# Weight tiles in three buffers instead of two, and the first output projection by halves of the sequence

## The reference, cut to what matters

```python
# block 1 (even): conformer convolution and a gated linear recurrence
z = h @ w_in;  va, vg, ga, xb, gb = split(z)
y_a = silu(layernorm(depthwise_conv31(va * sigmoid(vg)))) * silu(ga)
y_b = rglru(xb) * silu(gb)
x = x + gate * (concatenate([y_a, y_b]) @ w_out)       # w_out: 2048 x 1024
h = modulate(rmsnorm(x))
# block 2 (odd): multiscale pooling, grouped projection, output projection in two parts; rmsnorm
# block 3: gated linear attention, output projection, a gated projection of p ("ple")
# block 4 (fox): q, k, v, g = split(h @ w_in), 16 heads of 64;
logits = q.k / 8 + c[t] - c[s], causal;  o = softmax(logits) @ v, * silu(g), output projection, ple
```

## Time and profile before

| | |
|---|---|
| median of 3 runs | 3277.76 us (3275.65 to 3282.16) |
| the profiled execution | 3278.82 us, of which the profile's span is 3277.1 us |
| PE busy | 3028.1 us, 92% |
| DVE, ACT, POOL busy | 1759.4, 1061.4, 1216.6 us |
| granted TensorE clock | 0.965 of full speed |

### The profile page before, as it was taken

How to read it: one execution, slowest core, us unless ns; L and a number is a source line. 1 busy time by engine, 2 the same in 40 slices (tenths; PEclk the granted TensorE clock), 3 DMA queues, 4 the chain that set the end, 5 groups by cost and what they waited for, 6 DMA issues and landing times.

```text
span 3277.1 us, 39825 instructions
## 1 busy us (share of the span) xinstructions
PE 3028.1 (92%) x13850; PEld 2299.4 (70%) x13850; DVE 1759.4 (54%) x2248; ACT 1061.4 (32%) x1356; POOL 1216.6 (37%) x1466
## 2 busy tenths in 40 slices
PE   7999999979979999989889999998999999998997
PEld 1588777747868877767678877776666666665775
DVE  2499999984163415363632232445455555556353
ACT  3244334440021100000322232224455556655332
POOL 0244445414434433435423233675211212121575
PEclk9999999989989999989899999999999999998999
DMA  8212111243211131113211112333322122211323
GB/s 327 94 55 77 61 61 61 67 162 127 70 33 52 45 135 52 45 35 119 90 59 32 33 33 88 96 89 113 71 52 34 39 52 46 47 39 39 128 82 112
DMA packets 94241, 249.98 MB, mean 76 GB/s; under 512 B 24016, under 2 KB 25104, under 8 KB 92576
## 3 DMA queue, kind: packets, MB, share of 16 engines
q1 hardware_dynamic: 69520, 181.04, 19.1%
q10 hardware_dynamic: 24592, 67.21, 5.6%
HBM read 215.58 MB, written 32.64 MB: 76 GB/s over the span
## 4 chain that ended last, share of the span: by engine, by line
PE 63%; DVE 15%; issue 10%; ACT 6%; POOL 3%; DMA 1%; DVEq 1%; SPq 0%; POOLq 0%; ACTq 0%
PE ps L547 16%; PE ps L549 15%; PE ps L548 15%; DVE ps L1837 3%; POOL t_wl L505 2%; PE ps L1005 2%; PE ps L638 2%; DVE t_tt L1789 1%; PE ps L1022 1%; PE ps L819 1%; PE ps L821 1%; PE ps L820 1%; POOL t_wh L500 1%; DVE t_pr L2271 1%; PE ps L1042 1%
## 5 line engine op out<-in xcount | busy, mean ns | idle before, releaser
L547 PE MATMUL ps<-t_h_hi,t_wh 128*128 128x512 f32 x2464 | 1015.4, 412 | 69.1 <-POOLq L508 31.7
L500 POOL CAST t_wh<-t_wst 128x1024 fp32r<-128x1024 f32 (+2 forms) x290 | 314.8, 1085 | 1920.9 <-PE ps L549 1724.7
L548 PE MATMUL ps<-t_h_lo,t_wh 128*128 128x512 f32 x2464 | 984.0, 399 | 0.0
L549 PE MATMUL ps<-t_h_hi,t_wl 128*128 128x512 f32 x2464 | 982.7, 399 | 0.0
L505 POOL TENSOR_TENSOR t_wl<-t_wst,t_wh 128x256 fp32r<-128x256 f32 (+2 forms) x1160 | 895.5, 803 | 23.2
L547 PEld LDWEIGHTS ps<-t_h_hi,t_wh 128*128 128x128 f32 x2464 | 470.4, 191 | 216.3 <-issue 96.5
L549 PEld LDWEIGHTS ps<-t_h_hi,t_wl 128*128 128x128 f32 x2464 | 469.6, 191 | 115.9
L548 PEld LDWEIGHTS ps<-t_h_lo,t_wh 128*128 128x128 f32 x2464 | 470.6, 191 | 111.4 <-issue 7.5
L1837 DVE SCALAR_TENSOR_TENSOR ps<-t_upad,t_vec,ps 128x1024 f32<-128x1024 f32 x224 | 274.4, 1283 | 7.4 <-DVE ps L1833 1.1
L547 PE MATMUL ps<-t_y_hi,t_wh 128*128 128x512 f32 x512 | 207.6, 405 | 22.2 <-DVEq L247 14.6
L549 PE MATMUL ps<-t_y_hi,t_wl 128*128 128x512 f32 x512 | 205.2, 401 | 0.0
(11 more groups left out here) (343 smaller groups left out, 4255.1 us busy)
## 6 DMA issues: line engine op xcount, KB each, us to landing
t_modw<-w_mod SPq DMA_DIRECT2D x12, 2048.0 KB, 8.5
t_wst<-w_even_in SPq DMA_DIRECT2D x40, 512.0 KB, 3.5
t_wst<-w_ple SPq DMA_DIRECT2D x64, 320.0 KB, 2.9
t_wst<-w_fox_in SPq DMA_DIRECT2D x32, 512.0 KB, 3.6
t_xr<-x_d ACTq DMA_DIRECT2D x6, 2048.0 KB, 11.5
t_wst<-w_gla_in SPq DMA_DIRECT2D x24, 512.0 KB, 3.7
t_wst<-w_even_out SPq DMA_DIRECT2D x16, 512.0 KB, 3.5
x_d<-t_xr ACTq DMA_DIRECT2D x16, 512.0 KB, 2.6
```

What stands on the lines that cost most here:

```text
L500: pool.tensor_copy(wh[b][:, 0:w], wst[b][:, 0:w]).then_inc(S("w_high"), 1)
L547: pe.matmul(o, w1, x1, start=start and k == 0, stop=False)
L548: pe.matmul(o, w1, x2, start=False, stop=False)
L549: last = pe.matmul(o, w2, x1, start=False, stop=stop and k == kts - 1)
```

## The change

Tile n now has buffer n mod 3, and there are three pairs of buffers: `wst` with `wl` in the same place, and `wh` (24 KB as before). SP loads tile n, and POOL splits it, once PE is done with tile n-3. Where three does not divide a group's rounds, the loops of SP, POOL and PE are written out (`LOOPED` lists those that stay loops); in block 4 the wait in `load_tile` changes with the rest and the order of SP's program does not. The first output projection runs by halves, 32 tiles in the order `EVEN_OUT` (kind 0 is `y_b`, 1 is `y_a`; then the half and the output tile), with banks 2 to 7 of PSUM and bank 0 for the results and banks 0 and 1 for sums. `uc` lies by halves. The scans and the product of the last round move in among its taps, ACT takes the square roots of the last round ahead of the Silu of `ga`, and `y_b` is loaded in four steps. Layer norm, residual, squares and RMS norm are done once per half (on ACT and DVE in the same order, on 512 columns).

```diff
+EVEN_OUT = [(0, 0, m) for m in range(7)] + [(1, 0, m) for m in range(7)] + \
+    [(kind, 0, 7) for kind in range(2)] + [(kind, 1, m) for m in range(8) for kind in range(2)]
+LOOPED = ("w_even_in", "w_odd_in_a", "w_odd_in_b", "w_gla_in")
+BY_HALF = ("w_even_out", "w_odd_out_b", "w_gla_out", "w_ple_0", "w_fox_out", "w_ple_1")
 ...
-    wst = [sb(f"wst{i}", 1024, base + i * 4 * KB) for i in range(2)]
-    wh = [sb(f"wh{i}", 1024, base + (2 + i) * 4 * KB, F32R) for i in range(2)]
-    wl = [sb(f"wl{i}", 1024, base + (4 + i) * 4 * KB, F32R) for i in range(2)]
+    wst = [sb(f"wst{i}", 1024, base + 2 * i * 4 * KB) for i in range(3)]
+    wh = [sb(f"wh{i}", 1024, base + (2 * i + 1) * 4 * KB, F32R) for i in range(3)]
+    wl = [sb(f"wl{i}", 1024, base + 2 * i * 4 * KB, F32R) for i in range(3)]
 ...
     def wbuf(name, j):
 
-        return (first[name] + j) % 2
+        return (first[name] + j) % 3
 ...
-            sp.wait_ge(S("w_split"), first[name] + before + j + i * len(widths) + 1)
-            if name == "w_fox_in":
-                sp.sem_inc(S("sp_waited"), 1)
-            b = wbuf(name, j)
+            n = first[name] + before + j + i * len(widths)
+            if not isinstance(n, int) or n > 2:
+                sp.wait_ge(S("w_used"), n)
+            b = wbuf(name, before + j if name in LOOPED else before + j + i * len(widths))
             sp.dma_start(wst[b][:, 0:w],
 ...
-            pool.wait_ge(S(f"w_loaded{b}"),
-                         ((first[name] + before + j) // 2 + 1) * 16 + i * (len(widths) * 8))
-
-            pool.wait_ge(S("w_used"), n + 1)
+            if name in LOOPED:
+                pool.wait_ge(S(f"w_loaded{b}"), ((first[name] + j) // 3 + 1) * 16 + i * (len(widths) // 3 * 16))
+            else:
+                pool.wait_ge(S(f"w_loaded{b}"), (n // 3 + 1) * 16)
+            if not isinstance(n, int) or n > 2:
+                pool.wait_ge(S("w_used"), n)
             pool.sem_inc(S("pool_begun"), 1)
             pool.tensor_copy(wh[b][:, 0:w], wst[b][:, 0:w]).then_inc(S("w_high"), 1)
             pool.wait_ge(S("w_high"), n + 1)
 ...
+        def ln_sums(ks):
+            for k in ks:
+                pe.wait_ge(S("e_uc"), k + 2)
+                for c in range(2):
+                    last = pe.matmul(bank(c), ones, uch(c, k), start=(k == 0), stop=(k == KT - 1))
+            return last
+        def ln_var(c):
+            for k in range(KT):
+                pe.wait_ge(S("ln_sq"), 8 * c + k + 1)
+                pe.matmul(bank(c), ones, th(k % 2), start=(k == 0), stop=(k == KT - 1)).then_inc(S("ln_var"), 1)
+        def operand_ready(kind, c, k):
+            if kind == 1:
+                pe.wait_ge(S("ya_ready"), 8 * c + k + 1)
+            elif k == KT - 1:
+                pe.wait_ge(S("e_yl"), 8)
+            else:
+                pe.wait_ge(S(("yb_loaded", "yb_more", "yb_last", "yb_last")[k // 2] if c == 0 else "yb_last"), 32 + 32 * c)
+        def even_out(kind, c, m, ks=range(KT)):
+            n, t = EVEN_OUT.index((kind, c, m)), 8 * c + m
+            if kind == 0 and t > 6:
+                half_added("eout", t - 6)
+            if kind == 0 and t == 6:
+                pe.wait_ge(S("ln_rs"), 1)
+            pe.wait_ge(S("w_split"), first["w_even_out"] + n + 3)
+            last = project(wbuf("w_even_out", n), None, *((h_hi, h_lo), (y_hi, y_lo))[kind],
+                           chunks=[(c * HALF, HALF, out_bank("eout", t))], start=(kind == 0), stop=(kind == 1),
+                           ready=lambda k: operand_ready(kind, c, k), ks=ks)
+            if ks[-1] == KT - 1:
+                last.then_inc(S("w_used"), 1)
+        pe.wait_ge(S("e_evac"), 8 * 8 + 7)
+        ln_sums(range(KT - 1))
+        pe.wait_ge(S("e_evac"), 8 * 8 + 8)
+        for k in range(KT):
+            for m in range(2):
+                even_out(0, 0, m, (k,))
+        ln_sums(range(KT - 1, KT)).then_inc(S("ln_sum"), 1)
+        for m in (2, 3):
+            even_out(0, 0, m)
+        ln_var(0)
+        for m in (4, 5, 6):
+            even_out(0, 0, m)
+        for k in range(KT):
+            for m in range(2):
+                even_out(1, 0, m, (k,))
+        for m in (2, 3):
+            even_out(1, 0, m)
+        ln_var(1)
+        for m in (4, 5, 6):
+            even_out(1, 0, m)
+        for c in range(2):
+            for m in range(0 if c else 7, 8):
+                if c == 1 and m == 1:
+                    half_stats("eout", 0)
+                for kind in range(2):
+                    even_out(kind, c, m)
 ...
+                    two_tiles("eout", nm, [(wbuf(nm, 0), 0), (wbuf(nm, 1), 2)], lambda c: half_added("eout", 12 + c))
 ...
-        with pe.Fori(0, 3) as i:
-            window(2 * i + 1, 1, 1)
-            window(2 * i + 2, 0, 2)
+        for p in range(1, 7):
+            window(p, p % 2, 2 - p % 2)
 ...
+            def roots():
+                for d in range(2):
+                    act.wait_ge(S("e_q"), 2 * h + d + 1)
+                    A(tt[d][:, :], tt[d][:, :], ACT.Sqrt).then_inc(S("e_sqrt"), 1)
+            if last:
+                roots()
 ...
+        load_yb(0, 0, 2, "yb_loaded")
+        load_yb(0, 2, 4, "yb_more")
+        load_yb(0, 4, KT - 1, "yb_last")
+        act.wait_ge(S("yb_last"), 32)
+        load_yb(1, 0, KT - 1, "yb_last")
 ...
+        def ln_squares(c):
+            for k in range(KT):
+                act.wait_ge(S("ln_centered"), 8 * c + k + 1)
+                if 8 * c + k >= 2:
+                    act.wait_ge(S("ln_var"), 8 * c + k - 1)
+                A(th(k % 2), uch(c, k), ACT.Square).then_inc(S("ln_sq"), 1)
+            for k in range(2):
+                if c:
+                    act.wait_ge(S("ya_gated"), 7 + k)
+                ga_load(c, k)
+        def ln_apply(c):
+            act.wait_ge(S("ln_var"), 8 * c + 8)
+            rsqrt(xs_half(c), bank(c), D, eps5).then_inc(S("ln_rs"), 1)
+            for k in range(KT + 2):
+                if k < KT:
+                    act.wait_ge(S("ln_scaled"), 8 * c + k + 1)
+                    A(uch(c, k), uch(c, k), ACT.Silu, bias=V("ln_b", k), scale=V("ln_g", k)).then_inc(S("ln_silu"), 1)
+                if 1 <= k <= KT:
+                    act.wait_ge(S("ya_gated"), 8 * c + k)
+                    A(hcol(y_hi, c, k - 1), uch(c, k - 1), ACT.Copy).then_inc(S("ya_high"), 1)
+                    if k + 1 < KT:
+                        ga_load(c, k + 1)
+                if k >= 2:
+                    act.wait_ge(S("ya_ready"), 8 * c + k - 1)
+                    act.dma_start(xh(c, k - 2), dram["xT"][(k - 2) * P:(k - 1) * P, c * HALF:(c + 1) * HALF])\
+                        .then_inc(S(f"x_half{c}"), 16)
 ...
+        ln_squares(0)
+        ln_apply(0)
+        ln_squares(1)
+        act.wait_ge(S("ln_var"), 16)
+        for t in range(3):
+            squares_of("eout", t)
+        ln_apply(1)
         act.sem_inc(S("o_act"), 8)
-        high({"stat": 1, "op": 1, "bufs": 3, "layer": 1})
-        act.wait_ge(S("n_high"), 16)
-        act.wait_ge(S("x_stored"), 16 * 8)
+        for t in range(3, 16):
+            squares_of("eout", t)
+            if t == 7:
+                store_x(0, 0, 8)
+            if t == 8 + min(AT_TILE):
+                half_rs("eout", 0)
+            for k in AT_TILE.get(t - 8, []):
+                half_high("eout", 0, k)
+            if t == 11:
+                store_x(1, 0, 4)
+        store_x(1, 4, 8)
+        half_rs("eout", 1)
+        for k in range(KT):
+            half_high("eout", 1, k)
 ...
+        def last_result(h, i):
+            drive(h, i)
+            line.sync()
+            for d in range(2):
+                scan(d)
+            result(h)
+        def last_low(h, i):
+            dve.wait_ge(S("e_yh"), 8)
+            TT_(col(h_lo, 7), yb[:, :], col(h_hi, 7).bitcast(F32), ALU.subtract).then_inc(S("e_yl"), 1)
+        even_head(None, LRU_AT)
+        line.repeat(6, 6 + 4 + 1 + 1 + TAPS + 4, lambda i: even_head(i, LRU_AT))
+        even_head(6, {7: times_u, 12: low, 18: q, 23: last_result, 26: last_low})
 ...
+        def even_added(t):
+            c, m = divmod(t, 8)
+            half_residual("eout", "w_even_out", c, m, lambda m: mod(0, 0, 2, m))
+            half_square("eout", c, m, bank(1) if c else xs_half(0))
+            if m == 7:
+                summed()
+            if c == 1 and m in AT_TILE:
+                if m == min(AT_TILE):
+                    half_rs("eout", 0)
+                norm_tiles("eout", 0, AT_TILE[m], lambda k: gsc[:, 16 + k:17 + k], xs_half(0))
+        dve.wait_ge(S("ln_sum"), 1)
+        center(0)
+        ln_apply(0)
+        center(1)
+        for t in range(3):
+            even_added(t)
+        ln_apply(1)
+        for t in range(3, 16):
+            even_added(t)
+        half_rs("eout", 1)
+        norm_tiles("eout", 1, range(KT), lambda k: gsc[:, 16 + k:17 + k], xs_half(1))
```

(52 more changed lines are left out.)

275 lines of the change are left out of this document (110 added, 165 removed).

## The result

The changed kernel takes **3389.8 us** (median of 4 runs, 3381.0 to 3393.0) against 3278.4 (3275.7 to 3282.2): ratio 1.0335, 95% interval 1.0322 to 1.0347. It is slower, as forecast, but by 111 us and not by 39, and outside the range.

What follows compares the result with a forecast made beforehand. PE, busy 92% of the span, bounds the kernel by its work and gaps. 3278.8 - 27 (first projection) - 11 (third tiles) - 3 (ple phases) + 80 (block 4) = 3317.8, or 3317 us beside the median; range 3280 to 3345.

Steps and rivals of the forecast that it cites:

- the first half's maxima: Block 4 windows: their load, queued behind a newly waiting load, comes 13.4 us later for DVE; PE loses 10.4 a window.
- upper bound of 101: Block 4, seven windows: loss of 7 x 14.4 if DVE's whole delay and 1 us of clock show; 80 us expected.
- the maxima of the second half: Block 4 windows: late by some 2.6 us because the load of j=3 waits for step 4; about 0.7 shows.
- the sum of the first half is complete at 811, PE wants it at 807: 3.6: First output projection: PE waits 3.6 us for the first half's sum of squares, after residuals and second-half scaling.
- a gain under 15: Sign of being wrong: the first output projection gains less than 15 us, where 27 was forecast (bounds 15 and 36).
- the walk: First output projection, loss by loss: some 22 us plus 3 allowed, against 52 lost before, so 27 us gained.
- The rounds of block 1: Block 1's eight rounds: DVE holds the period, so the third buffer gains 0 of some 4.6 us.
- Third tiles and ple phases: Third buffer: 11.0 us gained at third tiles (lower bound 6 if PE waits for its other input), 3 in ple phases.
- two rules weighed: Skill rules judged against the trace: a DMA's fixed cost of about 2.0 us, and DVE/GpSimd locking their shared port pair.
- POOL left with 5 us of 22: First output projection: under the port-lock rule, DVE's 24 operations leave POOL one split instead of four, losing 6 us more.
- the maxima are not late: Rival, block 4: the maxima land before 2532.6, so PE does not wait and the kernel is faster, 3238; chance 0.13.
- in part: Rival, block 4: the delay shows only about 5 us a window because other waits shrink, 3273; chance 0.07.

Runs made afterwards that it cites:

- late-split run: Changed kernel with both halves' maxima stored and loaded early, POOL's splits in block 1, GLA phase and block 4 held back as with two buffers: 3274.2 us.
- the sum later: Changed kernel with both halves' maxima early, PE taking the first half's sum of squares one tile later in the first output projection: 3267.1 us.

## Why the prediction was right in direction and wrong in size

The measured loss is 73 us above the forecast. By steps of the sum: 5 in the first half's maxima, 22 in the second half's, 8 in the windows beside these, 20 in the first projection, 9 in block 1 and 12 in the GLA phase, less 2 or 3 at the third tiles and the ple phases.

**Block 4, the mechanism: right.** The load of j=2 waits for the last projection, the store 0.45 us behind it, DVE late by 14.1 where 13.4 stood, and the wait alone costs all of the 114. The first half's share was 10.7 a window in my sum and measures 80.3 / 7 = 11.5. How PE would spend it was off: 8 us at `scores(1)` but 1 instead of 3 at `values(0)`, with the lower clock making up for it. The windows as a whole, 114.8, lie above even the upper bound of 101.

**Block 4, the failed step: the maxima of the second half, late by some 2.6 us, "of which about 0.7 show".** They cost 26.6 / 7 = 3.8. A DVE idle of 2 us (the row at 2601.82) becomes a wait of PE at the values (26.6 us in all once the first half is cured) and lets the clock fall earlier, ahead of the squares. With 4.9 booked this is 21.7 of the 73 us that were missing. Another 8 come with the early splits, beside which PE waits longer for the squares; the late-split run took them down to 1.7. By which instructions they reach the squares stays open.

**The first output projection: the failed step is "the sum of the first half is complete at 811, PE wants it at 807: 3.6".** It is complete at 834.8. I had ACT and DVE do three residuals in front of the second half's scaling, and did not see that the squares stand in ACT's queue behind the second variance, which PE delivers only at about 784. The scaling of the second half then took 28.5 us and ended at 821.5, where I had about 800. With the low clock behind it the step cost 13 us (10 to 15, as this stretch scatters) where 3.6 were booked, as "the sum later" showed: about half of the 20 us missing here. The forecast had made a gain under 15 a sign of being wrong, and 7.3 is one. My addition was off as well: the losses of the walk come to 23 to 25, not to "some 22". The other walk points held: 6.5 for `y_b` (7.9), 3.8 for `uc` (4.7). PE's wait for POOL at `y_a`, 4.2 and 1.6, was underrated too (1 or 2); no run isolates it.

**The rounds of block 1, booked at 0 since "DVE holds the period".** DVE does hold it, and for that reason the answer was wrong. A split that starts when its load lands falls more beside the scans and less beside the taps, and DVE's own instructions get longer: +8.9. I had the two prices of a contended split and the contended 1.455 before me and used them in the projection only.

**The GLA phase was not in the sum: +12.1.** I listed what SP's moved loads pass in SP's own queue, and not what lands on the same engines from another: ACT's 8 KB, which take 3.4 us in place of 1.6 when they go out 0.35 us behind the 512 KB.

**Third tiles and ple phases: 14 forecast, 16.8 measured.** The third tile of block 2 gave little (-1.3 up to the last result): its 3.87 come back as new waits for DVE's pooling, the lower bound that I had named. The ple stretches gave more.

Of the two rules weighed, the fixed cost that the Trainium skill (DMA: Bandwidth & Descriptors, "Anatomy of one DMA") gives does not hold for these stores: 9.0 us for 2 KB in the list after, 8.4 before. That section gives the figure for transfers that GpSimd issues, and these go through SP's queue. That they are slow by their short elements fits the rows, and no run tests it. The lock of the port pair for a whole instruction, as the Trainium skill (SBUF — State Buffer, "Who interferes with whom") has it, agrees with the traces, and I was wrong to say that "both give way". Beside a scan of 2.65 us a quarter of a split took 2.72 in place of 0.74, seven times alike. Beside operations of half length the two engines take turns: DVE's go from 0.68 to 1.22 us and POOL's quarters from 0.70 to about 1.17 (four in 4.5 us, 2.8 alone). What did not follow is the price that I drew from it, POOL left with 5 us of 22, since neither engine is always first.

Of the rivals, "the maxima are not late" is refuted by the rows and by the wait put alone into the kernel before; "in part" as well. POOL does bound the first projection on two buffers (18.4 us of waits), on three only a little (8.4).

## What to carry to other kernels

When a load is made to wait for something later, walk every transfer that stands behind it in its queue, and then every small transfer of the other queues that lands in the same microseconds: 8 KB cost 12 us here beside 512 KB, and the wait for them had cost 10 before without them. Where an engine holds a period, its instructions' durations are themselves a function of what its neighbour does at that moment; moving the neighbour's work is not free even if it has slack. And a gap of PE is to be priced with the products that follow it at half the clock.

## What the runs showed of the hardware that I had not expected

- A wait of PE of 4.0 us in front of four small products cost 6.4 us of the head's period, one of 2.1 us some 3.1 (9.2 / 3).
- Two stores of 4-byte elements and the load of `negc` that went out just behind a needed load made PE wait 3.7 us more per window in the mean (79.1 against 53.3 us over seven), from 0.4 in one to 9.5 in another.
- DVE and POOL hold each other up by whole instructions where DVE reads SBUF alone (a quarter of a split 2.72 us beside a scan, 0.74 beside taps). Instructions of DVE with an operand in PSUM are spared: taps 1283 ns with early and with late splits, scans 1806 against 1540.
